# Hybrid Hyena and pooling encoder layer: the LayerNorm's gain and bias move from VectorE to GpSimd in the last stage

## The chip, the cores and the metric

The kernel runs on one core of a Trainium2 chip. The metric is the device time of one execution in microseconds (us), the median over runs. The engines named below are PE (TensorE, the matrix products), PEld (its weight loads), DVE (VectorE), ACT (ScalarE), POOL (GpSimd) and SP (SyncE, which issues the DMAs here).

## The reference

One encoder layer over x of 2048 x 1024 in fp32. One input projection feeds two branches, a two-fold gated long convolution and a pooling mixer; their outputs `y` (2048 x 1024) are mapped by one output matrix, gated, added to the scaled input, and normalised per row:

```python
ALPHA = DEEPNORM_ALPHA                      # 2 ** 0.25
def _layer_norm(x, g, b):
    mu = jnp.mean(xf, axis=-1, keepdims=True)
    var = jnp.mean(jnp.square(xf - mu), axis=-1, keepdims=True)
    y = (xf - mu) * lax.rsqrt(var + LN_EPS)
    return y * g + b
...
out = gate[:, None, :] * (y @ w_out[layer] + b_out[layer])
h = _layer_norm(DEEPNORM_ALPHA * h + out, ln_g[layer], ln_b[layer])
```

The change concerns only this last step.

## The kernel before

The layer runs in stages, each a block of its own with its buffers and semaphores: filters, input projection, three passes of a long convolution done as Fourier products, and at the end `last_inverse` and `output_norm`. Every product of two fp32 matrices is done as three products of parts (`mm3`, L150 to L152): a high part, and a low part that is what the high one leaves.

`output_norm` (from L1898) works on 16 tiles of 128 rows (tokens) by 1024 columns. Nearly every buffer is there twice, indexed by the tile number modulo 2. For tile n:

- ACT makes the high parts of `y` (`yhi`, `high`, L1975 and L1978), DVE the low parts (`ylo`, `low`, L1999 and L2002), each in two halves of 512 columns. They may overwrite the buffers once PE has finished tile n − 2.
- PE does 48 products into `ps` (`unit`): 24 that need the first half, then 24 that need the second.
- DVE makes `res` = ALPHA · x + gate bias beforehand (`skip`, L2009), and after PE's last product of the tile runs `norm`: it adds `ps` to `res` (L2025), takes the row statistics (L2029, L2032), then L2036 makes (res − mean) · ln_g while ACT takes the square root (`root`, L1983); five small instructions of one column (L2040 to L2044) refine the reciprocal, and L2048 makes o = res · rstd + ln_b.
- SP loads x (L1932) and stores `o` (L1944).

There is no scheduler: each engine's order is written out by `pipeline`, which walks over the tiles in bodies of four and gives for each body the steps with their lag. On DVE it is `[(low, 0), (skip, 0), (norm, 1)]`: low(n), skip(n), norm(n − 1), low(n + 1), and so on; behind the last tile only norms are left. On ACT it is high(n), root(n − 2), on SP load(n), store(n − 2). Waits are on semaphores only: `skip` waits for x and for `o_done` of tile n − 2 (since `res` is then free), the last instruction of `norm` also for the store of tile n − 2. POOL does one memset in this stage (`eps`, L1990). In the stage before, POOL makes the low part of the output weights (`whl`, L1867), and in the projection that of the input weights (L664, L666); these are the places where the trace shows POOL doing work of 128x1024.

Of the kernel before, what the change touches and what calls it, by code (L numbers as in the profile page):

```python
# [10 lines left out]
ALU = mybir.AluOpType  # L11
# [10 lines left out]
GS = L // P  # L22
# [132 lines left out]
def f32(ap):  # L155
    return ap.bitcast(F32)
# [9 lines left out]
def after(eng, sem, count):  # L166

    if not (isinstance(count, int) and count <= 0):
        eng.wait_ge(sem, count)


U = 4


def at(it, b, ring):

    it, b = it + b // U, b % U
    return b % ring, (U // ring) * it + b // ring


def pipeline(eng, units, steps, peel=(0,)):

    bodies = units // U
    steps = [step if len(step) == 3 else (*step, 2) for step in steps]
    first = max(1, *(-(-(lag + start) // U) for _, lag, start in steps))
    steps = [step[:2] for step in steps]

    def body(it, count=U):  # L190
        for b in range(count):
            for step, lag in steps:
                if not isinstance(it, int) or 0 <= U * it + b - lag < units:
                    step(it, b - lag)

    it = 0
    while it < bodies:
        if it < first or it in peel:
            body(it)
            it += 1  # L200
            continue
        end = min([p for p in peel if p > it] + [bodies])
        with eng.Fori(it, end) as i:
            body(i)
        it = end
    body(bodies, max(lag for _, lag in steps))
# [1691 lines left out]
def output_norm(nc, t, ya, yp, whl, gate_bias, out):  # L1898

    with Scope(nc, "out") as s:  # L1900
# [4 lines left out]
        res = [s.sb(f"res{b}", [P, D]) for b in range(2)]  # L1905
        o = [s.sb(f"o{b}", [P, D]) for b in range(2)]
        ln_g = s.sb("ln_g", [P, D])
        ln_b = s.sb("ln_b", [P, D])
        stats = [s.sb(f"stats{b}", [P, 2, 6]) for b in range(2)]
        mv = [s.sb(f"mv{b}", [P, 2]) for b in range(2)]  # L1910
        sm = [s.sb(f"sm{b}", [P, 4]) for b in range(2)]
        eps = s.sb("eps", [P, 1])
        ps = [s.ps(f"ps{b}", [P, 2, CH]) for b in range(2)]
        consts, eps_set = s.sem("consts"), s.sem("eps_set")
        yb_in = s.sems("yb_in", 4)
        x_in, hi_done, lo_done, mm_done, step, skip_done, sum_done, var_done, root_done, scaled, o_done, stored = (
            s.sems(n) for n in ("x_in", "hi_done", "lo_done", "mm_done", "step", "skip_done", "sum_done", "var_done",
                                "root_done", "scaled", "o_done", "stored"))
        block = s.block()

        @block.sync
        def _(sp):
            def load_yb(c):
                cols = slice(c * CH, (c + 1) * CH)
                sp.dma_start(yb[:, :, cols], yp[:, :, cols].rearrange("k p t -> p k t")).then_inc(yb_in[c], 16)

            def load(it, b):
                r, used = at(it, b, 2)
                after(sp, skip_done[r], used)
                row = P * (U * it + b)  # L1930
                src = t["x"][0, row:row + P, :] if isinstance(it, int) else t["x"][0, bass.ds(row, P), :]
                sp.dma_start(x[r][:, :], src).then_inc(x_in[r], 16)  # L1932
                if isinstance(it, int) and U * it + b == 1:
                    sp.dma_start(ln_g[:, :], t["ln_g"][0, :].partition_broadcast(P)).then_inc(consts, 16)
                    sp.dma_start(ln_b[:, :], t["ln_b"][0, :].partition_broadcast(P)).then_inc(consts, 16)
                    for c in range(1, 4):
                        load_yb(c)

            def store(it, b):
                r, used = at(it, b, 2)  # L1940
                sp.wait_ge(o_done[r], used + 1)
                row = P * (U * it + b)
                dst = out[0, row:row + P, :] if isinstance(it, int) else out[0, bass.ds(row, P), :]
                sp.dma_start(dst, o[r][:, :]).then_inc(stored[r], 16)  # L1944

            load_yb(0)
            pipeline(sp, GS, [(load, 0), (store, 2)])
            for r in range(2):
                sp.wait_ge(stored[r], 16 * GS // 2)
# [38 lines left out]
        @block.gpsimd  # L1988
        def _(pool):
            nc.gpsimd.memset(eps[:, :], LN_EPS).then_inc(eps_set, 1)  # L1990

        @block.vector
        def _(dve):
            def low(it, b):
                r, used = at(it, b, 2)
                cols = bass.ds(P * (U * it + b), P)
                dve.wait_ge(hi_done[r], 2 * used + 1)
                after(dve, mm_done[r], used)
                nc.vector.tensor_tensor(ylo[r][:, 0:4, :], ya[:, :, cols],  # L1999
                                        f32(yhi[r][:, 0:4, :]), ALU.subtract).then_inc(lo_done[r], 1)  # L2000
                dve.wait_ge(hi_done[r], 2 * used + 2)
                nc.vector.tensor_tensor(ylo[r][:, 4:8, :], yb[:, :, cols],  # L2002
                                        f32(yhi[r][:, 4:8, :]), ALU.subtract).then_inc(lo_done[r], 1)

            def skip(it, b):
                r, used = at(it, b, 2)
                dve.wait_ge(x_in[r], 16 * used + 16)
                after(dve, o_done[r], used)
                nc.vector.scalar_tensor_tensor(out=res[r][:, :], in0=x[r][:, :], scalar=ALPHA, in1=gate_bias[:, :],  # L2009
                                               op0=ALU.mult, op1=ALU.add).then_inc(skip_done[r], 1)  # L2010

            def norm(it, b):
                r, used = at(it, b, 2)
                STEPS = 6
                n = STEPS * used
                done = [0]

                def then(ins):
                    ins.then_inc(step[r], 1)
                    done[0] += 1  # L2020
                    dve.wait_ge(step[r], n + done[0])

                dve.wait_ge(skip_done[r], used + 1)
                dve.wait_ge(mm_done[r], used + 1)
                nc.vector.tensor_tensor(res[r][:, :], ps[r][:, :, :].rearrange("p a b -> p (a b)"), res[r][:, :],  # L2025
                                        ALU.add).then_inc(sum_done[r], 1)
                dve.wait_ge(sum_done[r], used + 1)
                for h in range(2):
                    ins = nc.vector.bn_stats(stats[r][:, h, :], res[r][:, h * CH:(h + 1) * CH])  # L2029
                then(ins)  # L2030
                nc.vector.memset(sm[r][:, 2:4], 0.0)
                nc.vector.bn_aggr(mv[r][:, :], stats[r][:, :, :].rearrange("p a b -> p (a b)")).then_inc(var_done[r], 1)  # L2032
                dve.wait_ge(var_done[r], used + 1)
                if isinstance(it, int) and U * it + b == 0:
                    dve.wait_ge(consts, 32)
                nc.vector.scalar_tensor_tensor(out=res[r][:, :], in0=res[r][:, :], scalar=mv[r][:, 0:1], in1=ln_g[:, :],  # L2036
                                               op0=ALU.subtract, op1=ALU.mult).then_inc(scaled[r], 1)
                dve.wait_ge(root_done[r], used + 1)

                then(nc.vector.reciprocal(sm[r][:, 1:2], sm[r][:, 0:1]))  # L2040
                then(nc.vector.tensor_scalar(sm[r][:, 2:3], mv[r][:, 1:2], LN_EPS, sm[r][:, 1:2], ALU.add, ALU.mult))  # L2041
                then(nc.vector.tensor_tensor(sm[r][:, 2:3], sm[r][:, 2:3], sm[r][:, 1:2], ALU.mult))  # L2042
                then(nc.vector.tensor_scalar(sm[r][:, 2:3], sm[r][:, 2:3], -0.5, 1.5, ALU.mult, ALU.add))  # L2043
                then(nc.vector.tensor_tensor(sm[r][:, 3:4], sm[r][:, 2:3], sm[r][:, 1:2], ALU.mult))  # L2044
                assert done[0] == STEPS
                dve.wait_ge(scaled[r], used + 1)
                after(dve, stored[r], 16 * used)
                nc.vector.scalar_tensor_tensor(out=o[r][:, :], in0=res[r][:, :], scalar=sm[r][:, 3:4], in1=ln_b[:, :],  # L2048
                                               op0=ALU.mult, op1=ALU.add).then_inc(o_done[r], 1)

            pipeline(dve, GS, [(low, 0), (skip, 0), (norm, 1)])


# [60 lines left out]
```

## Time and profile before

| | |
|---|---|
| median of 3 runs | 1349.3 us (1344.42, 1349.3, 1350.38) |
| the profiled execution | 1344.42 us, its span 1342.6 us |
| busy over the span | PE 1119.0, PEld 857.6, DVE 861.3, ACT 532.1, POOL 149.1 us |
| `output_norm` | from about 1148 us to the end of the span |
| in it, 1160 to 1310 us | PE 150.00 of 150 us busy, DVE 109.14, ACT 20.25, POOL 0 |
| last store issued | 1338.57 us |

A time of the timeline is the start of an instruction from the span's start and its length. On DVE the next instruction's start lies some 0.08 us before the end of the one in front, so the step from start to start is what an instruction costs there. A bracket behind a row is idle time before it and what ended it. An instruction that is held up once it has started shows this as a longer duration, not as idle time.

### The profile page before, as it was taken

Reading aid. Unit: us, or ns where it says so; the run is one execution under the profiler, and the core shown is the slowest. Engines: PE = TensorE matmul, PEld = TensorE weight load, DVE = VectorE, ACT = ScalarE, POOL = GpSimd, SP = SyncE. Lnnn points to the kernel's source line nnn. Section 1 sums busy time; section 2 is a strip of 40 time slices with the busy share of each in tenths; the row PEclk is TensorE's granted clock in tenths of the full one; section 3 lists DMA queues with packets and bytes.
Section 4 is the critical chain, followed back from the end, with each engine's and each line's share of the span. In section 5 each row is a group of like instructions: output and inputs, shape, how many; then the busy total and the mean of one; then the engine's idle time right before and its main releaser. Section 6 shows DMA issues by size and latency. Waiting matters only on the chain. (4 is left out here: it accounts for less than half of the span.)

```text
span 1342.6 us, 14415 instructions
## 1 busy us (share of the span) xinstructions
PE 1119.0 (83%) x4940; PEld 857.6 (64%) x4940; DVE 861.3 (64%) x1037; ACT 532.1 (40%) x722; POOL 149.1 (11%) x98
## 2 busy tenths in 40 slices
PE   3789746999999799969888499976999646899996
PEld 1257534788888577657666377754777434688885
DVE  5969659555545165548778355644888538577776
ACT  3347635333433133336565333333666435111110
POOL 0011044111111111111100111101110014100000
PEclk9879957999999799979999799997999869899999
DMA  8369998687653246587787567767798598622221
GB/s 299 111 207 354 317 253 279 206 267 260 214 189 115 71 130 194 172 209 230 234 238 231 152 175 228 244 214 206 232 276 257 161 373 282 235 94 94 94 94 47
DMA packets 156337, 276.56 MB, mean 206 GB/s; under 512 B 24743, under 2 KB 46375, under 8 KB 154154
## 3 DMA queue, kind: packets, MB, share of 16 engines
q1 hardware_dynamic: 151773, 269.60, 62.9%
q0 software_dynamic: 3168, 5.51, 1.5%
q8 instruction: 37, 0.61, 0.2%
q10 hardware_dynamic: 1328, 0.59, 0.2%
q14 instruction: 31, 0.25, 0.1%
HBM read 183.37 MB, written 98.57 MB: 210 GB/s over the span
## 5 line engine op out<-in xcount | busy, mean ns | idle before, releaser
L150 PE MATMUL prj_pp<-prj_uhi,prj_whi 128*128 128x512 f32 x768 | 308.6, 402 | 14.9 <-POOL prj_ulo L1044 8.7
L152 PE MATMUL prj_pp<-prj_uhi,prj_wlo 128*128 128x512 f32 x768 | 304.7, 397 | 0.0
L151 PE MATMUL prj_pp<-prj_ulo,prj_whi 128*128 128x512 f32 x768 | 304.6, 397 | 0.0
L150 PEld LDWEIGHTS prj_pp<-prj_uhi,prj_whi 128*128 128x128 f32 x768 | 147.5, 192 | 57.0 <-issue 25.4
L152 PEld LDWEIGHTS prj_pp<-prj_uhi,prj_wlo 128*128 128x128 f32 x768 | 146.7, 191 | 32.5
L151 PEld LDWEIGHTS prj_pp<-prj_ulo,prj_whi 128*128 128x128 f32 x768 | 147.0, 191 | 31.7
L150 PE MATMUL out_ps<-whl,out_yhi 128*128 128x512 f32 x256 | 102.5, 400 | 4.3 <-DVE out_ylo L1999 4.3
L151 PE MATMUL out_ps<-whl,out_yhi 128*128 128x512 f32 x256 | 102.2, 399 | 0.0
L152 PE MATMUL out_ps<-whl,out_ylo 128*128 128x512 f32 x256 | 102.1, 399 | 0.0
L664 POOL CAST prj_whi<-prj_ws 128x1024 fp32r<-128x1024 f32 x24 | 28.3, 1180 | 611.5 <-PE prj_pp L152 518.0
L1165 DVE TENSOR_TENSOR p_alo<-p_a,p_ahi 128x1024 fp32r<-128x1024 f32 x32 | 45.4, 1419 | 74.5 <-ACT p_ahi L1105 74.4
L1105 ACT ACTIVATE p_ahi<-p_a 128x1024 fp32r<-128x1024 f32 x32 | 33.9, 1060 | 118.0 <-PE p_ps L152 103.0
L1486 ACT ACTIVATE p_us<-p_u 64x512 f32<-64x512 f32 x64 | 38.1, 595 | 91.6 <-PE p_u L152 52.2
L150 PE MATMUL p_u<-p_ahi,p_fwd 128*128 128x512 f32 x64 | 28.9, 451 | 45.9 <-DVE p_alo L1528 29.7
L666 POOL TENSOR_TENSOR prj_wlo<-prj_ws,prj_whi 128x1024 fp32r<-128x1024 f32 x24 | 60.2, 2506 | 1.9
L150 PEld LDWEIGHTS out_ps<-whl,out_yhi 128*128 128x128 f32 x256 | 48.6, 190 | 16.4 <-DVE out_ylo L1999 4.5
L694 ACT ACTIVATE prj_row<-prj_pp,prj_b_in 128x512 f32<-128x512 f32 x64 | 43.4, 679 | 37.8 <-PE prj_pp L152 37.8
L535 PE MATMUL fs_s<-fs_khi,fs_tab 64*128 64x512 f32 x256 | 50.7, 416 | 7.7 <-ACT fs_xo L576 7.7
L1975 ACT ACTIVATE out_yhi<-ya 128x512 fp32r (+1 forms) x16 | 10.1, 631 | 117.6 <-PE out_ps L152 114.1
L151 PEld LDWEIGHTS out_ps<-whl,out_yhi 128*128 128x128 f32 x256 | 48.7, 190 | 12.0
L152 PEld LDWEIGHTS out_ps<-whl,out_ylo 128*128 128x128 f32 x256 | 48.7, 190 | 11.9
L1555 DVE TENSOR_TENSOR p_us<-p_us,p_k_im 128x1024 f32<-128x1024 f32 x32 | 39.2, 1226 | 20.6 <-ACT p_us L1487 20.6
(180 smaller groups left out, 2076.2 us busy)
## 6 DMA issues: line engine op xcount, KB each, us to landing
kseq<-fs_xo SPq DMA_DIRECT2D x32, 512.0 KB, 5.2
p_a<-kseq SPq DMA_DIRECT2D x32, 512.0 KB, 4.4
kfreq<-p_out SPq DMA_DIRECT2D x32, 512.0 KB, 5.2
xseq<-p_xo SPq DMA_DIRECT2D x32, 512.0 KB, 6.5
p_a<-xseq SPq DMA_DIRECT2D x32, 512.0 KB, 5.7
p_k_re<-kfreq SPq DMA_DIRECT2D x64, 256.0 KB, 4.1
p_k_im<-kfreq SPq DMA_DIRECT2D x64, 256.0 KB, 4.5
bseq<-p_out SPq DMA_DIRECT2D x32, 512.0 KB, 4.8
```

Source lines behind the costliest of these rows:

```text
L150: nc.tensor.matmul(out, w[0], m[0], start=start, stop=False, skip_group_check=True)
L151: nc.tensor.matmul(out, w[0], m[1], start=False, stop=False, skip_group_check=True)
L152: return nc.tensor.matmul(out, w[1], m[0], start=False, stop=stop, skip_group_check=True)
L535: mm = nc.tensor.matmul(s1_ps[r][:, jj, :], tab[g % 3][js, h, a, :], m[r3][js, h, :], start=h == 0 and part == 0, stop=h == 1 and part == ...
L664: self.nc.gpsimd.tensor_copy(self.whi[b][:, :, :], self.ws[:, :, :]).then_inc(self.whi_done[b], 1)
L666: self.nc.gpsimd.tensor_tensor(self.wlo[b][:, :, :], self.ws[:, :, :], f32(self.whi[b][:, :, :]), ALU.subtract).then_inc(self.wlo_done[b], 1)
L694: self.nc.scalar.activation(self.row[:, PAD + c * CH:PAD + (c + 1) * CH], self.pp[q % 2][:, :], ACT.Identity, bias=self.b_in[:, col:col + ...
L1105: nc.scalar.activation(ahi[:, :, :], a[n % 2][:, :, :], ACT.Copy).then_inc(hi_done, 1)
L1165: nc.vector.tensor_tensor(alo[:, :, :], a[n % 2][:, :, :], f32(ahi[:, :, :]), ALU.subtract).then_inc(lo_done, 1)
L1486: nc.scalar.activation(us[0:64, i, :], u_ps[64:128, i, :], ACT.Copy, scale=-1.0)
L1555: nc.vector.tensor_tensor(us[:, :, :], us[:, :, :], k_im[:, :, :], ALU.mult).then_inc(turn_done, 1)
L1975: nc.scalar.activation(yhi[r][:, 0:4, :], ya[:, :, cols], ACT.Copy).then_inc(hi_done[r], 1)
```

## The change

Of the four factors of (res − mean) · rstd · ln_g + ln_b, DVE keeps the first two in one instruction, tensor_scalar in place on `res` with the two column operands mean and rstd, and raises the new semaphore `norm_done`. POOL multiplies by ln_g into `o` (raises `scaled`), waits for its own multiply, and adds ln_b in place (raises `o_done`). The two scalar_tensor_tensor instructions of DVE are gone. POOL takes over the wait for the constants and for the store of tile n − 2. `skip` waits for `scaled` (POOL has read `res`) and no longer for `o_done`.

```diff
         @block.gpsimd
         def _(pool):
             nc.gpsimd.memset(eps[:, :], LN_EPS).then_inc(eps_set, 1)
+            pool.wait_ge(eps_set, 1)
+            pool.wait_ge(consts, 32)
+            for n in range(GS):
+                b, it = n % 2, n // 2
+                pool.wait_ge(norm_done[b], it + 1)
+                after(pool, stored[b], 16 * it)
+                nc.gpsimd.tensor_tensor(o[b][:, :], res[b][:, :], ln_g[:, :], ALU.mult).then_inc(scaled[b], 1)
+                pool.wait_ge(scaled[b], it + 1)
+                nc.gpsimd.tensor_tensor(o[b][:, :], o[b][:, :], ln_b[:, :], ALU.add).then_inc(o_done[b], 1)
@@ skip
                 dve.wait_ge(x_in[r], 16 * used + 16)
-                after(dve, o_done[r], used)
+                after(dve, scaled[r], used)
@@ norm
                 nc.vector.bn_aggr(mv[r][:, :], stats[r][:, :, :].rearrange("p a b -> p (a b)")).then_inc(var_done[r], 1)
-                dve.wait_ge(var_done[r], used + 1)
-                if isinstance(it, int) and U * it + b == 0:
-                    dve.wait_ge(consts, 32)
-                nc.vector.scalar_tensor_tensor(out=res[r][:, :], in0=res[r][:, :], scalar=mv[r][:, 0:1], in1=ln_g[:, :],
-                                               op0=ALU.subtract, op1=ALU.mult).then_inc(scaled[r], 1)
                 dve.wait_ge(root_done[r], used + 1)
...
-                dve.wait_ge(scaled[r], used + 1)
-                after(dve, stored[r], 16 * used)
-                nc.vector.scalar_tensor_tensor(out=o[r][:, :], in0=res[r][:, :], scalar=sm[r][:, 3:4], in1=ln_b[:, :],
-                                               op0=ALU.mult, op1=ALU.add).then_inc(o_done[r], 1)
+                nc.vector.tensor_scalar(res[r][:, :], res[r][:, :], mv[r][:, 0:1], sm[r][:, 3:4],
+                                        ALU.subtract, ALU.mult).then_inc(norm_done[r], 1)
```

DVE, one tile of `output_norm` before, from the statistics of tile n − 1 to the sum of tile n (`sm` holds the small columns, `mv` mean and variance):

```order
L2032 BN_AGGR out_mv<-out_stats 128x2
L2036 SCALAR_TENSOR_TENSOR out_res<-out_res,out_mv,out_ln_g 128x1024
L2040 RECIPROCAL out_sm<-out_sm 128x1
L2041 TENSOR_SCALAR out_sm<-out_mv,out_sm 128x1
L2042 TENSOR_TENSOR out_sm<-out_sm 128x1
L2043 TENSOR_SCALAR out_sm<-out_sm 128x1
L2044 TENSOR_TENSOR out_sm<-out_sm 128x1
L2048 SCALAR_TENSOR_TENSOR out_o<-out_res,out_sm,out_ln_b 128x1024
L1999 TENSOR_TENSOR out_ylo<-ya,out_yhi 128x512
L2002 TENSOR_TENSOR out_ylo<-out_yb,out_yhi 128x512
L2009 SCALAR_TENSOR_TENSOR out_res<-out_x,gate_bias 128x1024
L2025 TENSOR_TENSOR out_res<-out_ps,out_res 128x1024
```

The same piece of DVE's order in the changed kernel, whose lines lie 9 further down where the text is the same up to the statistics:

```order
L2041 BN_AGGR out_mv<-out_stats 128x2
L2044 RECIPROCAL out_sm<-out_sm 128x1
L2045 TENSOR_SCALAR out_sm<-out_mv,out_sm 128x1
L2046 TENSOR_TENSOR out_sm<-out_sm 128x1
L2047 TENSOR_SCALAR out_sm<-out_sm 128x1
L2048 TENSOR_TENSOR out_sm<-out_sm 128x1
L2050 TENSOR_SCALAR out_res<-out_res,out_mv,out_sm 128x1024
L2008 TENSOR_TENSOR out_ylo<-ya,out_yhi 128x512
L2011 TENSOR_TENSOR out_ylo<-out_yb,out_yhi 128x512
L2018 SCALAR_TENSOR_TENSOR out_res<-out_x,gate_bias 128x1024
L2034 TENSOR_TENSOR out_res<-out_ps,out_res 128x1024
```

Between the statistics and the reciprocal nothing stands any more; the tensor_scalar stands where L2048 stood, with the low halves and the skip product right behind it.

POOL, in the same stage, the first two tiles of the changed kernel and what is in front:

```order
L1990 MEMSET out_eps 128x1
L1997 TENSOR_TENSOR out_o<-out_res,out_ln_g 128x1024
L1999 TENSOR_TENSOR out_o<-out_o,out_ln_b 128x1024
L1997 TENSOR_TENSOR out_o<-out_res,out_ln_g 128x1024
L1999 TENSOR_TENSOR out_o<-out_o,out_ln_b 128x1024
```

Before, the memset was all; now 32 instructions of 128x1024 follow it.

## Rows read from the trace of the kernel before

**Rows 1.** 1160 to 1310 us: length, PE, PEld, DVE, ACT, POOL busy, clock, DMA

```profile
1160.00:1310.00 150.00, 150.00 (x644) 120.49 (x643) 109.14 (x196) 20.25 (x41) 0.00 (x0) 1.00 0.32 112
```

**Rows 2.** waits, 1010 to 1343 us: engine, line, releaser, total, times, longest

```profile
DVE out_res L2025 <- PE out_ps L152: 45.5, 16, 5.7
...
PE out_ps L150 <- DVE out_ylo L1999: 4.3, 1, 4.3
```

**Rows 3.** timeline of DVE, one tile: start us, us, engine, line, shapes, [idle before]

```profile
1265.02 1.22 DVE L2025 TENSOR_TENSOR out_res<-out_ps,out_res 128x1024 f32<-128x1024 f32 x1 [2.53 <-PE out_ps L152]
...
1267.60 0.20 DVE L2032 BATCH_NORM_AGGREGATE out_mv<-out_stats 128x2 f32<-128x12 f32 x1
...
1267.84 1.29 DVE L2036 SCALAR_TENSOR_TENSOR out_res<-out_res,out_mv,out_ln_g 128x1024 f32<-128x1024 f32 x1
1269.04 0.16 DVE L2040 RECIPROCAL out_sm<-out_sm 128x1 f32<-128x1 f32 x1
...
1270.06 1.29 DVE L2048 SCALAR_TENSOR_TENSOR out_o<-out_res,out_sm,out_ln_b 128x1024 f32<-128x1024 f32 x1
1271.26 0.69 DVE L1999 TENSOR_TENSOR out_ylo<-ya,out_yhi 128x512 fp32r<-128x512 f32 x1
1271.86 0.68 DVE L2002 TENSOR_TENSOR out_ylo<-out_yb,out_yhi 128x512 fp32r<-128x512 f32 x1
1272.47 1.22 DVE L2009 SCALAR_TENSOR_TENSOR out_res<-out_x,gate_bias 128x1024 f32<-128x1024 f32 x1
1276.21 1.22 DVE L2025 TENSOR_TENSOR out_res<-out_ps,out_res 128x1024 f32<-128x1024 f32 x1 [2.53 <-PE out_ps L152]
```

**Rows 4.** timeline of ACT, same tile: the square root

```profile
1267.84 0.29 ACT L1983 ACTIVATE out_sm<-out_mv,out_eps 128x1 f32<-128x1 f32 x1 [1.64 <-DVE out_mv L2032]
```

**Rows 5.** one line's instructions, L392: duration ns min/median/max

```profile
L392 DVE TENSOR_SCALAR net_arg<-net_arg x6: 693/694/694, 21.4 to 57.9; 128x1024 f32<-128x1024 f32 x6
```

**Rows 6.** the same view for L712

```profile
L712 DVE TENSOR_SCALAR prj_cv<-prj_row,prj_cw,prj_cb x48: 531/541/2419, 223.1 to 1044.0; 128x512 f32<-128x512 f32 x48
```

**Rows 7.** timeline of POOL at the end of the stage before, L1867

```profile
1139.64 3.21 POOL L1867 TENSOR_TENSOR whl<-fin_wf,whl 128x1024 fp32r<-128x1024 f32 x1 [3.39 <-ACT whl L1858]
1145.09 2.37 POOL L1867 TENSOR_TENSOR whl<-fin_wf,whl 128x1024 fp32r<-128x1024 f32 x1 [2.25 <-ACT whl L1858]
```

**Rows 8.** page, part 5: POOL's two-input instructions of the projection

```profile
L666 POOL TENSOR_TENSOR prj_wlo<-prj_ws,prj_whi 128x1024 fp32r<-128x1024 f32 x24 | 60.2, 2506 | 1.9
```

**Rows 9.** timeline of DVE, the last tile

```profile
1332.21 1.23 DVE L2025 TENSOR_TENSOR out_res<-out_ps,out_res 128x1024 f32<-128x1024 f32 x1 [4.87 <-PE out_ps L152]
...
1337.26 1.28 DVE L2048 SCALAR_TENSOR_TENSOR out_o<-out_res,out_sm,out_ln_b 128x1024 f32<-128x1024 f32 x1
```

**Rows 10.** timeline of all engines, the end: the last store

```profile
1338.57 0.34 SPq L1944 DMA_DIRECT2D out<-out_o  x1
```

**Rows 11.** timeline of DVE around 1140 us, beside POOL of rows 7

```profile
1139.38 1.21 DVE L1876 TENSOR_TENSOR fin_xlo<-fin_x,fin_xhi 128x1024 fp32r<-128x1024 f32 x1
1140.51 1.08 DVE L1884 TENSOR_TENSOR ya<-fin_tps,ya 128x512 f32<-128x512 f32 x1
1141.49 2.43 DVE L1892 TENSOR_TENSOR fin_wf<-fin_wf,fin_gate 128x1024 f32<-128x1024 f32 x1
```

**Rows 12.** timeline of all engines at 660 us: POOL and DVE take turns

```profile
660.39 1.22 DVE L1528 TENSOR_TENSOR p_alo<-p_a,p_ahi 128x1024 fp32r<-128x1024 f32 x1
...
660.44 2.06 POOL L664 CAST prj_whi<-prj_ws 128x1024 fp32r<-128x1024 f32 x1 [37.22 <-PE prj_pp L152]
...
661.52 1.26 DVE L712 TENSOR_SCALAR prj_cv<-prj_row,prj_cw,prj_cb 128x512 f32<-128x512 f32 x1
...
662.58 2.47 POOL L666 TENSOR_TENSOR prj_wlo<-prj_ws,prj_whi 128x1024 fp32r<-128x1024 f32 x1
...
662.82 2.78 DVE L715 SCALAR_TENSOR_TENSOR prj_cv<-prj_row,prj_cw,prj_cv 128x512 f32<-128x512 f32 x1
```

**Rows 13.** DMA issues, 1145 to 1343 us: KB each, median us to landing

```profile
out_x<-in_x SPq DMA_DIRECT2D x16, 512.0 KB, 3.9
```

More of the change, by code:

```diff
@@ L1915, in output_norm @@
         yb_in = s.sems("yb_in", 4)
-        x_in, hi_done, lo_done, mm_done, step, skip_done, sum_done, var_done, root_done, scaled, o_done, stored = (
+        x_in, hi_done, lo_done, mm_done, step, skip_done, sum_done, var_done, root_done, norm_done, scaled, o_done, stored = (
             s.sems(n) for n in ("x_in", "hi_done", "lo_done", "mm_done", "step", "skip_done", "sum_done", "var_done",
-                                "root_done", "scaled", "o_done", "stored"))
+                                "root_done", "norm_done", "scaled", "o_done", "stored"))
         block = s.block()
```

## The prediction, made before the changed kernel was run

> **What bounds the kernel now.** The change touches only the last stage, so I first read the busy time of that stage. From 1160 to 1310 us TensorE is busy for all of the 150.00 us, at a granted clock of 1.00 (2.4 GHz), VectorE for 109.14 and POOL for none [rows 1]. Then the list of waits: in the whole stage PE waited once for VectorE's low halves, 4.3 us, at the start (`ylo`, L1999), while VectorE waited 16 times, 45.5 us in all, for PE's product [rows 2]. So the stage goes at PE's pace. The timeline of VectorE gives this pace: the sum of one tile (L2025) starts at 1265.02 and that of the next at 1276.21, 11.19 us a tile, the last 2.53 us of them idle [rows 3]. What can move the end is (a) what stands behind PE's last product, since nothing hides it, and (b) VectorE's loop, if it needs more than 11.19 us a tile for long enough that PE waits for `ylo`. The first is a plain sum. The second is close, and decides how far above the sum the result lies.
>
> **The serial part of a tile on VectorE, before.** I call S the start of a tile's sum. The square root on ACT and the removed L2036 both start at S + 2.82 (1267.84 less 1265.02) [rows 3, 4]. The five small instructions from L2040 to L2044 take 1270.06 − 1269.04 = 1.02 us [rows 3].
>
> **Removed.** Two instructions a tile, L2036 and L2048, 1.29 us each, 1.20 from start to start [rows 3]. L2036 covered the square root: that took 0.29 [rows 4], so it was ready long before 1269.04. Without the cover the reciprocal waits for it: it starts at about S + 2.82 + 0.29 + 0.04 for the signal (0.04 is also what lay between the end of L2032, 1267.80, and ACT's start [rows 3, 4]) = S + 3.15, and the small ones end at S + 4.17.
>
> **Added on VectorE.** One tensor_scalar of 128x1024, in place, one tensor in, two [128,1] operands. The trace has no such form. The nearest rows are the same width with constants, 0.694 us [rows 5], and half the width with two column operands, 0.541 [rows 6]. Twice the width costs a two-input instruction 1.22 − 0.68 = 0.54 us more [rows 3]; L392 does 1024 elements in what those need for 512, so it goes at twice their rate, and I add 0.27: 0.54 + 0.27 = 0.81. I take 0.80. From below it is bounded by 0.69, from above by the 1.29 of the removed form. So it ends at S + 4.97, where the removed L2048 ended at S + 6.33.
>
> A rule that bears on this choice, of the Trainium skill, VectorE: DVE Perf Modes, "The perf-mode tier table": an fp32 tensor_scalar from SBUF to SBUF runs at two elements a cycle, and a tensor_tensor at one. L392 agrees with it, and by it the new instruction is nearer to 0.8 than to 1.29.
>
> **Added on POOL.** Two tensor_tensor of 128x1024 a tile, each behind a semaphore. POOL's own two-input instruction of this size took 2.37 us where nothing was in its way [rows 7]; the 24 of the projection averaged 2.51, waiting included [rows 8]. I take 2.37, and 2.37 to 2.5 as bounds. With about 0.06 for VectorE's signal and 0.09 between the two the pair ends 4.9 us behind the tensor_scalar.
>
> The Trainium skill, GPSIMD Engine Reference, "Performance versus the Vector engine", speaks against moving such work: a two-input elementwise instruction costs GpSimd about 2.6 cycles an element, and VectorE one. By its rate, 1024 x 2.6 / 1.2 GHz = 2.2 us (estimate from that page), the tail's +3.5 below would be +3.2; the row stands at 2.37, so it is used.
>
> **The tail (a), the main term.** Before, the last tile's sum starts at 1332.21, L2048 starts at 1337.26 and ends 1.28 later, 1338.54, so 6.33 us from S, and the store is issued at 1338.57 [rows 9, 10]. After: S + 4.97 + 0.06 + 2.37 + 0.09 + 2.37 = S + 9.86, and then the same store. Difference +3.5 us. Bounds: 0.69 and 2.37 give +3.4; 0.81 and 2.5 give +3.8. A tensor_scalar of 1.29 adds 0.5.
>
> **The loop (b).** What was hidden work becomes contention. Where POOL's two-input instruction meets a two-input instruction of VectorE, the trace shows one waiting for the whole of the other. At 1139.38 VectorE runs L1876 for 1.21; POOL's, begun at 1139.64, takes 3.21 instead of 2.37, so it ends 2.26 behind VectorE's end, at 1142.85; VectorE's next two-input one, L1892, begun at 1141.49, takes 2.43 instead of 1.22 and ends at 1143.92, 1.07 behind POOL's [rows 7, 11]. L1884 between them, whose one input is PSUM, ran beside POOL in 1.08 [rows 11]. And they take turns: around 660 us VectorE asks at 660.39, POOL at 660.44, VectorE at 661.52 with L712 (a tensor_scalar, 1.26 instead of 0.54), POOL at 662.58, VectorE at 662.82, and each gets its turn in this order [rows 12]. So even back-to-back instructions of VectorE let a waiting POOL in between.
>
> In the changed kernel what follows the tensor_scalar on VectorE is just of that kind: `ylo` first half, `ylo` second half, the skip product (both inputs in SBUF, 0.69, 0.68 and 1.22 [rows 3]). Counted from the tensor_scalar's end, with a blocked instruction ending its own time less 0.14 behind the other's end (2.37 − 2.23; 0.68 − 0.55; both rounded [rows 7, 11, 12]):
> - low half 1, already running: ends at +0.60
> - POOL's multiply, asked for meanwhile: +0.60 + 2.23 = +2.83
> - low half 2: +2.83 + 0.55 = +3.38
> - POOL's add, asked for at +2.9: +5.61
> - the skip product, which must also wait for the multiply, is behind the add: +5.61 + 1.08 = +6.69; the next sum can start 0.08 earlier, +6.61.
>
> A tile needs 4.97 + 6.61 = 11.58 us on VectorE, against PE's 11.19. So VectorE, which had 2.53 us to spare, falls back by 0.39 us a tile. That does not reach PE at once: PE's next tile needs the first `ylo` half, which is ready at S + 4.97 + 0.60 = S + 5.57, when VectorE is not late, and is wanted at S + 11.19: 5.62 us of room. The last tile that PE takes gets its `ylo` behind the norm of tile 13; by then VectorE is 13 x 0.39 = 5.1 us late. So PE just doesn't wait, by half a microsecond. At the end there are no more low halves and skips, and VectorE catches up: tile 14's norm ends 5.5 + 4.97 = 10.5 behind its product, before the last product at 11.19. But POOL's pair of tile 14 then lasts until about 4.1 us into the last tile's norm, where the small two-input instructions (L2042, L2044 before) may be blocked for up to 0.5 us. Term: 0 to +0.5, I take +0.2.
>
> **Others, at nothing.** The skip product's wait for `scaled` instead of `o_done` is inside the turns above. On SP the store moves later by some 4 us, and the load behind it; x takes 3.9 us to land [rows 13] and is used more than 9 us after its issue, so it stays hidden, and if that cover went, the skip product would be late by the difference. On ACT only the root is behind VectorE; the high halves wait for PE alone.
>
> **Sum.** 3.5 + 0.2 = +3.7 us. The profiled execution took 1344.42 us (span 1342.6, 1.8 outside it), so 1348.1 for it. That run is the lowest of the three shown; on the median of 1349.3 it is 1353.0, +0.27%. What a measurement of this kernel can tell from no change is about 0.5%, 6.7 us, so I forecast "no change that can be told", on the slow side.
>
> **Rivals.**
> - No queueing that counts: VectorE keeps the port through its back-to-back instructions, or POOL asks later. The loop is then 4.97 + 0.60 + 0.60 + 2.23 + about 1.2 = 9.6 us, below 11.19, and only the tail is left: +3.5, 1352.8. Against it: POOL got in between at 661.5 [rows 12].
> - The loop is longer than read, slower than before beyond what can be told (other side, the first of two sizes): each 0.1 us more a tile costs PE 1.3 us as soon as the lateness passes 5.62. With POOL at 2.5 the loop is 0.26 longer, 0.65 late a tile: 13 x 0.65 − 5.6 = 2.8 us of waiting PE, and with the pair at 2.5 and the blocking +7 in all, 1356. From 0.43 a tile on it decides. For it: the mean of 2.51 [rows 8]; against it: the undisturbed 2.37 [rows 7].
> - The tensor_scalar at the removed form's 1.29 us: loop 12.07, 0.88 late a tile, past 5.62 after seven tiles, 13 x 0.88 − 5.6 = 5.8 us of waiting PE; tail 3.5 + 0.5; POOL's pair of tile 14 blocks the small instructions for some 1.2 more: +11, 1360. For it: two column operands are only seen at 512. Against it: 0.541 there is less than the 0.68 of a one-rate instruction [rows 3, 6].
> - Faster: PE has no gap to give back and the tail only grows, so only run-to-run difference would show it (1344.4 to 1350.4 in the runs shown).
>
> **How the numbers follow.** Forecast, +3.5 to +5: 0.52. First rival 0.15. Longer loop, +5 to +10: 0.18. Slow tensor_scalar, +11 or more: 0.10. The rest 0.05. Below 6.7 us lie the forecast, the first rival and a bit of the third: with the runs' own spread, same 0.70; slower 0.26; faster 0.04. The range goes from 1348 (tail alone on a run as low as the profiled one) to 1360 (slow tensor_scalar on the median).
>
> **What would show it.** The norm's tensor_scalar at 0.80; POOL busy about 5 us a tile, more in the records since they hold its waiting; the second `ylo` half and the skip product of VectorE stretched to some 3 us and 3.5 us; VectorE's idle time before the sum gone, and the sum starting later behind the product from tile to tile, by about 0.4; PE still without waits; from the last sum to the store 9.9 us. Wrong would be: PE waiting for `ylo` in the second half of the stage (longer loop), idle time still before each sum (first rival), or a shorter tail.

## The result, and the profile after

| | before | changed |
|---|---|---|
| median | 1348.01 us (1342.95 to 1350.38, 8 runs) | 1354.88 us (1350.19 to 1357.9, 8 runs) |
| profiled execution | 1344.42 us, span 1342.6 | 1355.51 us, span 1353.7 |
| first sum of the last stage starts at | 1164.22 | 1170.51 |
| from there to the last sum | 167.99 | 168.87 |
| from the last sum to the last store's issue | 6.36 | 10.28 |
| from there to the end of the span | 4.03 | 4.04 |
| the stage: from the first sum to the end | 178.38 | 183.19 |

The ratio of the changed kernel to the one before is 1.0056, with a 95% interval of 1.0035 to 1.0077: slower, by about the least that can be told. The stage that was changed takes 4.8 us more, 0.36%. Of the 11.1 us between the two spans 6.3 stand ahead of the first sum, where the two programs are the same; the experiments show how far that time wanders by itself.

Busy time between 1160 and 1310 us in the changed kernel, with the columns of [rows 1]:

```profile
1160.00:1310.00 150.00, 150.00 (x641) 120.39 (x640) 136.27 (x173) 21.50 (x42) 66.12 (x24) 0.99 0.32 114
```

VectorE has two instructions of 128x1024 a tile fewer and one more, and is busy for 136 us instead of 109 [rows 1]. That is the first lesson of this text: busy time also counts the time for which an instruction is held. The waits of the last stage (who waited, for whom, us in all, times, longest):

```profile
DVE out_res L2034 <- PE out_ps L152: 6.1, 2, 5.4
...
PE out_ps L150 <- DVE out_ylo L2008: 4.5, 2, 4.3
```

Before each sum VectorE used to wait for PE, 45.5 us over 16 tiles [rows 2]. Now it waits twice: at the first and at the last tile. PE, on the other hand, has one wait more in the list than the 4.3 at the start. The chain of work that ended last ran mostly through PE before (PE 14% of the span, DVE 1%); now it runs mostly through VectorE:

```profile
DVE 9%; issue 3%; PE 2%; ACT 0%; DVEq 0%; POOL 0%; POOLq 0%
```

### The profile page after: what moved, and what is told of

It is laid out like the page before. It is cut to its first block and busy times, and to the rows that moved or that the text cites. A ratio compares the mean times of both kernels' runs of the same rounds, so it can differ in the third digit from the quotient of the medians.

```text
span 1353.7 us, 14426 instructions
## 1 busy us (share of the span) xinstructions
PE 1128.5 (83%) x4940; PEld 863.8 (64%) x4940; DVE 895.4 (66%) x1021; ACT 532.4 (39%) x722; POOL 234.9 (17%) x130
## 5 line engine op out<-in xcount | busy, mean ns | idle before, releaser
L1997 POOL TENSOR_TENSOR out_o<-out_res,out_ln_g 128x1024 f32<-128x1024 f32 x16 | 43.6, 2722 | 106.9 <-DVE out_res L2050 106.9
```

Of the source, the lines that this page charges most:

```text
L1997: nc.gpsimd.tensor_tensor(o[b][:, :], res[b][:, :], ln_g[:, :], ALU.mult).then_inc(scaled[b], 1)
```

## Where the 4.8 us are

One tile in the middle, the timeline of DVE and POOL together, answering to [rows 3]:

```profile
1193.84 1.21 DVE L2034 TENSOR_TENSOR out_res<-out_ps,out_res 128x1024 f32<-128x1024 f32 x1
...
1196.41 0.20 DVE L2041 BATCH_NORM_AGGREGATE out_mv<-out_stats 128x2 f32<-128x12 f32 x1
...
1196.98 0.16 DVE L2044 RECIPROCAL out_sm<-out_sm 128x1 f32<-128x1 f32 x1 [0.36 <-ACT out_sm L1983]
...
1198.00 0.81 DVE L2050 TENSOR_SCALAR out_res<-out_res,out_mv,out_sm 128x1024 f32<-128x1024 f32 x1
...
1198.73 0.68 DVE L2008 TENSOR_TENSOR out_ylo<-ya,out_yhi 128x512 fp32r<-128x512 f32 x1
1198.89 2.78 POOL L1997 TENSOR_TENSOR out_o<-out_res,out_ln_g 128x1024 f32<-128x1024 f32 x1 [6.07 <-DVE out_res L2050]
...
1199.33 2.90 DVE L2011 TENSOR_TENSOR out_ylo<-out_yb,out_yhi 128x512 fp32r<-128x512 f32 x1
...
1201.75 2.73 POOL L1999 TENSOR_TENSOR out_o<-out_o,out_ln_b 128x1024 f32<-128x1024 f32 x1
...
1202.15 3.42 DVE L2018 SCALAR_TENSOR_TENSOR out_res<-out_x,gate_bias 128x1024 f32<-128x1024 f32 x1
...
1205.49 1.21 DVE L2034 TENSOR_TENSOR out_res<-out_ps,out_res 128x1024 f32<-128x1024 f32 x1
```

Read the durations against [rows 3]: the second `ylo` half takes 2.90 instead of 0.68, the skip product 3.42 instead of 1.22. POOL's multiply asks at 1198.89, while the first half runs, gets in when that is done at 1199.41 and ends 2.26 later; the second half, asked for at 1199.33, ends 0.56 behind it; then the add, then the skip product. From sum to sum it is 11.66 us (1205.49 less 1193.84, with rounding), PE's pace being 11.20. There is no idle time before the sum. The tensor_scalar takes 0.81, and the reciprocal starts 3.14 us behind the sum.

So VectorE falls back by 0.46 us a tile, and near the end PE feels it. Tiles are counted from 0 here. The starts of PE's tiles 14 and 15, the last two, timeline of all engines:

```profile
1315.36 0.68 DVE L2008 TENSOR_TENSOR out_ylo<-ya,out_yhi 128x512 fp32r<-128x512 f32 x1
...
1315.60 0.39 PE L152 MATMUL out_ps<-whl,out_ylo 128*128 128x512 f32 x1
...
1316.10 0.50 PE L150 MATMUL out_ps<-whl,out_yhi 128*128 128x512 f32 x1
...
1327.00 0.69 DVE L2008 TENSOR_TENSOR out_ylo<-ya,out_yhi 128x512 fp32r<-128x512 f32 x1
...
1327.17 0.40 PE L152 MATMUL out_ps<-whl,out_ylo 128*128 128x512 f32 x1
...
1327.83 0.47 PE L150 MATMUL out_ps<-whl,out_yhi 128*128 128x512 f32 x1 [0.26 <-DVE out_ylo L2008]
```

Inside a tile PE's products start 0.23 us apart. The first of tile 14 starts 0.50 behind the one in front of it, just after the end of the `ylo` half that it needs (1316.04), and the second follows after 0.34. The first of tile 15 starts 0.66 behind the one in front, 0.14 after the end of its half (1327.69), and the second follows after 0.31. What is above 0.23 adds up to 0.27 + 0.11 + 0.43 + 0.08 = 0.89 us, and from the first to the last sum the stage is 0.88 us longer than before. So PE was held twice, and that is the whole of this part. The list of waits shows only 0.2 of it, because a product's record is 0.39 to 0.40 long, longer than the step to the next: as idle time a short hold shows too small or not at all.

The traces also say when the half is wanted. In the kernel before, the timeline of PE has the first product of the next tile at 1275.95, where the sum in [rows 3] starts at 1276.21. PE begins the next tile 0.26 us ahead of the sum of the one in front. The prediction had it wanting the half at the sum + 11.19, so the room for VectorE's lateness is not 5.62 us but 5.36. The half of tile 14 is made behind the norm of tile 12, and by then VectorE is 12 x 0.46 = 5.52 us late, past 5.36. For tile 13 it was 11 x 0.46 = 5.06, and PE wasn't held.

The last tile, timeline of all engines, answering to [rows 9], and SP's last store, answering to [rows 10]:

```profile
1339.38 1.23 DVE L2034 TENSOR_TENSOR out_res<-out_ps,out_res 128x1024 f32<-128x1024 f32 x1 [0.67 <-PE out_ps L152]
...
1341.21 2.34 POOL L1999 TENSOR_TENSOR out_o<-out_o,out_ln_b 128x1024 f32<-128x1024 f32 x1
...
1342.98 0.59 DVE L2046 TENSOR_TENSOR out_sm<-out_sm 128x1 f32<-128x1 f32 x1
...
1343.99 0.81 DVE L2050 TENSOR_SCALAR out_res<-out_res,out_mv,out_sm 128x1024 f32<-128x1024 f32 x1
1344.88 2.34 POOL L1997 TENSOR_TENSOR out_o<-out_res,out_ln_g 128x1024 f32<-128x1024 f32 x1 [1.33 <-DVE out_res L2050]
1347.30 2.34 POOL L1999 TENSOR_TENSOR out_o<-out_o,out_ln_b 128x1024 f32<-128x1024 f32 x1
```

```profile
1349.66 0.34 SPq L1944 DMA_DIRECT2D out<-out_o  x1
```

The tensor_scalar ends at the sum + 5.42, POOL's pair at + 10.26. One small instruction, L2046, has two inputs of one column in SBUF; it takes 0.59 instead of 0.16, held until the add of tile 14 ends at 1343.55. From the last sum to the last store's issue it is 3.92 us longer than before; I call this part the tail. 0.88 + 3.92 = 4.8.

## The experiments

Each ran beside the kernel before on the same chip (29 runs of it for e1 to e4, 23 for e5 to e7), with 12 runs of its own, e4 with 6 and e6 with 4. "The stage" is the time from the first sum to the end of the span, 178.4 before. It and the two columns in front are read from one profile of each; the changed kernel was profiled twice, with 183.2 and 183.3.

| run | from sum to sum | first to last sum | the stage | ratio to before (95%) |
|---|---|---|---|---|
| before | 11.20 | 168.0 | 178.4 | |
| changed | 11.66 | 168.9 | 183.2 | 1.0056 (1.0035 to 1.0077) |
| e1, changed again | 11.66 | 168.9 | 183.3 | 1.0025 (1.0006 to 1.0044) |
| e2, last tile on VectorE | 11.66 | 168.9 | 180.5 | 1.0019 (1.0002 to 1.0037) |
| e3, only the last tile on POOL | 11.20 | 168.0 | 182.1 | 1.0028 (1.0012 to 1.0044) |
| e4, multiply behind the low halves | 12.20 | 176.0 | 190.9 | 1.0086 (1.0051 to 1.0120) |
| e5, add behind the skip product | 11.20 | 168.0 | 182.0 | 1.0028 (1.0011 to 1.0046) |
| e6, one more tensor_scalar | 12.38 | 179.0 | 194.9 | 1.0115 (1.0086 to 1.0144) |
| e7, all on VectorE, split last tile | 11.20 | 167.9 (right half) | 177.0 | 0.9982 (0.9965 to 0.9998) |

**e1: the changed kernel again**, no edit.

> The changed kernel once more, beside the other variants. Theory A (what the traces show of the last stage is all): from the first sum to the issue of the last store it takes 179.2 us as in the first profile, before 174.4, so the kernel is 4.8 us slower, +0.36%, and the first sum's own time (1164.2 before, 1170.5 after in the two profiles) differs only from run to run. Rival B (the stages ahead of the change have become slower too, as the two profiles and the median difference of 6.9 us suggest): +0.5% or more again, and the first sum again some 6 us later than in before.

Median 1351.28 us of 12 runs, against 1347.94 of 29. The stage takes 183.3 us, to a tenth what it took the first time, while the first sum is back at 1165.0. Over the nine profiles of this text it started at 1163.3 to 1166.6, and twice at 1170.5 (in the changed kernel and in e6), in programs that are the same up to there. So nothing shows that the stages ahead became slower; the first measurement's 0.56% and this one's 0.25% lie on both sides of the stage's 0.36%, which is inside both intervals. What makes the time ahead of the stage wander stays open: the two profiles' mean granted clock was 0.928 before and 0.920 in the changed kernel, but over the 52 runs of the kernel before that stood beside the experiments, clock and time go together only loosely.

**e2: the last tile on VectorE.** POOL's loop runs over GS − 1 tiles, and `norm` of the last tile is the one before, with waits for POOL and for the store of tile 13 (cut here):

```diff
-            for n in range(GS):
+            for n in range(GS - 1):
@@ norm, last tile only
+                    nc.vector.scalar_tensor_tensor(out=res[r][:, :], in0=res[r][:, :], scalar=mv[r][:, 0:1], in1=ln_g[:, :],
+                                                   op0=ALU.subtract, op1=ALU.mult).then_inc(scaled[r], 1)
...
+                    nc.vector.scalar_tensor_tensor(out=o[r][:, :], in0=res[r][:, :], scalar=sm[r][:, 3:4], in1=ln_b[:, :],
+                                                   op0=ALU.mult, op1=ALU.add).then_inc(o_done[r], 1)
```

> Tiles 0 to 14 as in the changed kernel, the last tile's gain and bias on VectorE as before. Theory A: the loop of 11.66 us a tile stays, VectorE 5 to 6 us late at tile 14; from the last sum to the last store it takes not 10.3 but 6.3 plus about 1.2, since the two-input instruction with ln_g asks at the sum + 2.8 and POOL's add of tile 14 goes on until + 4.2: 7.5. So 2.7 us less than the changed kernel, first sum to store 176.5. Rival (the loss lies in the loop, VectorE's lateness, not in the tail): no gain over the changed kernel, first sum to store 178 to 179. Rival (no waiting behind POOL at the end): the tail is 6.3.

Timeline of all engines, the last tile:

```profile
1333.42 1.23 DVE L2034 TENSOR_TENSOR out_res<-out_ps,out_res 128x1024 f32<-128x1024 f32 x1 [0.64 <-PE out_ps L152]
...
1335.30 2.34 POOL L1999 TENSOR_TENSOR out_o<-out_o,out_ln_b 128x1024 f32<-128x1024 f32 x1
...
1336.25 2.47 DVE L2046 SCALAR_TENSOR_TENSOR out_res<-out_res,out_mv,out_ln_g 128x1024 f32<-128x1024 f32 x1
...
1339.66 1.28 DVE L2060 SCALAR_TENSOR_TENSOR out_o<-out_res,out_sm,out_ln_b 128x1024 f32<-128x1024 f32 x1
```

From the last sum to the last store's issue it is 7.5 us: the instruction with ln_g is held by POOL's add of tile 14 until 1337.64 and takes 2.47 instead of 1.28. The stage is 2.7 us shorter than the changed kernel's. The tail is real, and part of what is won by taking the last tile off POOL is lost because POOL is still at tile 14.

**e3: only the last tile on POOL**, the kernel before otherwise (the same edit the other way round).

> The kernel before, only the last tile's gain and bias on POOL. Theory A: no loop with turns, VectorE waits 2.5 us for PE at each tile as before; the last sum to the store takes 3.15 + 1.02 + 0.81 + 0.06 + 2.35 + 0.08 + 2.35 = 9.8 us, 3.5 more than before; first sum to store 177.9, time +3.5 us, +0.26%. Rival (loss in the loop): no slower than before.

Timeline of all engines, the last tile, sum and POOL's pair:

```profile
1334.61 1.22 DVE L2033 TENSOR_TENSOR out_res<-out_ps,out_res 128x1024 f32<-128x1024 f32 x1 [4.87 <-PE out_ps L152]
...
1339.84 2.34 POOL L1996 TENSOR_TENSOR out_o<-out_res,out_ln_g 128x1024 f32<-128x1024 f32 x1 [188.44 <-DVE out_res L2062]
1342.26 2.34 POOL L1998 TENSOR_TENSOR out_o<-out_o,out_ln_b 128x1024 f32<-128x1024 f32 x1
```

One tile out of 16 moved, and three quarters of the loss are there: 3.7 us of 4.8. From sum to sum it stays at 11.20. The pair ends 9.99 behind the sum, 0.2 more than expected.

**e4: the multiply behind the low halves.**

```diff
                 pool.wait_ge(norm_done[b], it + 1)
+                if n + 2 < GS:
+                    pool.wait_ge(lo_done[b], 2 * it + 4)
```

> The changed kernel, but POOL's multiply waits until VectorE has made both low halves of the tile two further on, so POOL no longer gets in between them. Theory A: the second low half takes 0.68 again; the skip product waits for the multiply (2.35, plus signals), the add runs beside the sum; the loop is 4.98 + 0.6 + 0.6 + 2.5 + 1.2 = 9.9 us a tile, below PE's 11.2, so VectorE is never late and has 1.3 us idle at each tile; nothing of POOL's tile 14 is left when the last norm's small instructions run; last sum to store 9.8, first sum to store 177.9: 1.3 us less than the changed kernel and like e3. Rival (VectorE's lateness costs nothing at all, everything is the tail): the same time as the changed kernel within 0.5 us. Rival (turns do not matter for the order): the second low half still takes 2.9.

This missed by far, and in the other direction: ratio 1.0086. Timeline of DVE and POOL, one tile:

```profile
1183.57 0.69 DVE L2013 TENSOR_TENSOR out_ylo<-out_yb,out_yhi 128x512 fp32r<-128x512 f32 x1
...
1184.40 2.39 POOL L1999 TENSOR_TENSOR out_o<-out_res,out_ln_g 128x1024 f32<-128x1024 f32 x1 [7.34 <-DVE out_ylo L2013]
...
1186.87 2.40 POOL L2001 TENSOR_TENSOR out_o<-out_o,out_ln_b 128x1024 f32<-128x1024 f32 x1
1186.90 3.45 DVE L2020 SCALAR_TENSOR_TENSOR out_res<-out_x,gate_bias 128x1024 f32<-128x1024 f32 x1 [2.64 <-POOL out_o L1999]
...
1190.28 1.21 DVE L2036 TENSOR_TENSOR out_res<-out_ps,out_res 128x1024 f32<-128x1024 f32 x1
```

The low halves are free again, 0.69. But the skip product has to wait for the multiply, and when that is done both engines ask again: POOL's add at 1186.87, VectorE's skip product at 1186.90. The add goes first, and the skip product takes 3.45; so it is at all 14 skip products that wait for a multiply, with the add 0.02 to 0.03 ahead. I had it the other way round. Half the turns are gone, yet the loop has become longer, 12.20, since the multiply no longer overlaps anything that VectorE can do. VectorE is then 1.00 late a tile, and PE waits for it nine times, at the start (4.3) and at each tile from tile 8 on:

```profile
PE out_ps L150 <- DVE out_ylo L2010: 10.2, 9, 4.3
```

**e5: the add behind the skip product.**

```diff
                 pool.wait_ge(scaled[b], it + 1)
+                if n + 2 < GS:
+                    pool.wait_ge(skip_done[b], it + 2)
```

> The changed kernel, but POOL's add waits until VectorE has made the skip product of the tile two further on. Theory A (a tile's loop on VectorE against PE's 11.20 us decides, and in e4 the loop was 12.20 because POOL's add, asking 0.02 us ahead of the skip product, still went first): the multiply gets in between the low halves, the second of them takes 2.9; the skip product takes 1.22 again, the add runs beside the sum. Loop 4.98 + 0.6 + 2.25 + 0.47 + 1.2 = 9.5 us, below 11.20: 1.7 us of idle time before each sum, PE never waits, first sum to last sum 168.0, last sum to the end of the store's issue 10.4 as in e3, span behind the first sum 182.1: 1.1 less than the changed kernel (183.2), 3.7 more than before (178.4). Rival (POOL's work costs by its amount, not by its turns): as the changed kernel, 183.2.

Timeline of DVE and POOL, one tile:

```profile
1192.02 2.78 POOL L1997 TENSOR_TENSOR out_o<-out_res,out_ln_g 128x1024 f32<-128x1024 f32 x1 [4.17 <-DVE out_res L2052]
...
1192.45 2.90 DVE L2013 TENSOR_TENSOR out_ylo<-out_yb,out_yhi 128x512 fp32r<-128x512 f32 x1
...
1195.27 1.21 DVE L2020 SCALAR_TENSOR_TENSOR out_res<-out_x,gate_bias 128x1024 f32<-128x1024 f32 x1
...
1196.62 2.42 POOL L2001 TENSOR_TENSOR out_o<-out_o,out_ln_b 128x1024 f32<-128x1024 f32 x1 [1.83 <-DVE out_res L2020]
...
1198.14 1.23 DVE L2036 TENSOR_TENSOR out_res<-out_ps,out_res 128x1024 f32<-128x1024 f32 x1 [1.66 <-PE out_ps L152]
```

The multiply still holds the second low half (2.90), the skip product is free (1.21), and the add runs beside the sum and the statistics, which it does not slow. VectorE waits 1.66 us for PE before the sum, PE never for VectorE, and the stage takes 182.0, the value of e3. The same amount of POOL's work, differently placed, costs nothing but the tail.

**e6: one more tensor_scalar in each norm**, in front of the one with mean and rstd:

```diff
+                then(nc.vector.tensor_scalar(res[r][:, :], res[r][:, :], 1.0, 0.0, ALU.mult, ALU.add))
```

> The changed kernel with one more tensor_scalar of 128x1024 with constants (times 1, plus 0) in each norm, about 0.7 us. Theory A (threshold: VectorE's loop minus 11.20 adds up until its lateness passes 5.6 us, then PE waits for it): loop 11.66 + 0.72 = 12.38, 1.18 late a tile, PE's first wait at the fifth or sixth tile, 13 x 1.18 - 5.6 = 9.7 us of waiting in all; tail + 0.72; span behind the first sum 183.2 + 9.7 - 0.3 + 0.7 + about 0.6 for more blocking at the end = 194. Rival (each tile's extra work counts at once): 16 x 0.72 = 11.5, 194.7, but then with PE waiting from the second tile on. Rival (VectorE hidden as before): + 0.7, 183.9.

The loop is 12.38 us. PE's waits in the stage, and the first of them behind the start that the list has, at tile 7:

```profile
PE out_ps L150 <- DVE out_ylo L2008: 12.8, 10, 4.3
```

```profile
1238.85 0.47 PE L150 MATMUL out_ps<-whl,out_yhi 128*128 128x512 f32 x1 [1.02 <-DVE out_ylo L2008]
```

By the steps between the products PE is held first at the start of tile 6 (1226.37, 0.42 behind the product in front instead of 0.23, too short for the list). That is a tile or two later than I had written. For six tiles the lateness costs nothing, then about all of it: the threshold of theory A. The totals can't tell it from the rival that counts each tile's work at once (194 and 194.7 expected, 194.9 measured); the waits can, since the rival had PE waiting from the second tile on.

My 9.7 us for PE's side was 1.3 short of the 11.0 measured, and the traces show where that lies. The added instruction stands in front of the low half too and takes 0.72 off the room; PE wants the half 0.26 earlier than I had it; and at the last hold the first product starts 0.14 behind the half and the second 0.08 late, as in the changed kernel. So the room is 5.36 − 0.72 = 4.64, and 13 x 1.18 − 4.64 + 0.22 = 10.9. The same sum gives 13 x 0.46 − 5.36 + 0.22 = 0.84 for the changed kernel, where 0.88 was measured, and 13 x 1.00 − 5.36 + 0.22 = 7.9 for e4, against 8.0. It also gives the first tile at which PE is held, 14, 8 and 6, as in the traces.

**e7: a version for the tail.** The experiments say that in this stage, as long as VectorE keeps PE's pace, only what stands behind PE's last product counts. So this version leaves all on VectorE, as before, and shortens that. PE's last four tiles are written out, so that the last one can be told apart; declarations and the code of the stores are left out here:

```diff
@@ unit, last tile: behind the left half's last product
+                            mm.then_inc(left_done, 1)
@@ norm, last tile
+                    for h, (sem, value) in enumerate(((left_done, 1), (mm_done[r], used + 1))):
+                        cols = slice(h * CH, (h + 1) * CH)
+                        dve.wait_ge(sem, value)
+                        nc.vector.tensor_tensor(res[r][:, cols], ps[r][:, h, :], res[r][:, cols],
+                                                ALU.add).then_inc(sum_done[r], 1)
+                        dve.wait_ge(sum_done[r], used + 1 + h)
+                        ins = nc.vector.bn_stats(stats[r][:, h, :], res[r][:, cols])
...
+                for cols in ((slice(0, CH), slice(CH, D)) if last else (slice(0, D),)):
+                    nc.vector.scalar_tensor_tensor(out=o[r][:, cols], in0=res[r][:, cols], scalar=sm[r][:, 3:4],
+                                                   in1=ln_b[:, cols], op0=ALU.mult, op1=ALU.add).then_inc(o_done[r], 1)
@@ store, last tile: two halves of the columns, each behind its o_done
```

> The kernel before, all on VectorE, but in the last tile the sum and the statistics of the left half of the columns are made as soon as PE has finished that half (12 products, 2.8 us, before its last), and the last instruction and the store go in two halves. Theory A (what stands behind PE's last product is all that can be won in this stage): the sum and statistics left behind the last product are half as long, 1.2 us less; the last instruction's halves cost 0.1 more together, and the store's second half lands a bit sooner than the whole: span behind the first sum 178.4 - 1.2 - 0 to 0.5 = 176.7 to 177.3, time -1 to -1.7 us, -0.1%, which the median can hardly tell but the trace can. Rival (the end is set by the store of 512 KB, not by VectorE): no gain.

Timeline of DVE and SP, the last tile:

```profile
1328.45 0.69 DVE L2037 TENSOR_TENSOR out_res<-out_ps,out_res 128x512 f32<-128x512 f32 x1 [2.07 <-PE out_ps L152]
...
1329.17 0.69 DVE L2040 BATCH_NORM_STATS2 out_stats<-out_res 128x6 f32<-128x512 f32 x1
...
1331.18 0.69 DVE L2037 TENSOR_TENSOR out_res<-out_ps,out_res 128x512 f32<-128x512 f32 x1 [1.31 <-PE out_ps L152]
1331.91 0.69 DVE L2040 BATCH_NORM_STATS2 out_stats<-out_res 128x6 f32<-128x512 f32 x1
...
1335.10 1.41 DVE L2067 SCALAR_TENSOR_TENSOR out_o<-out_res,out_sm,out_ln_b 128x512 f32<-128x512 f32 x2
1335.88 0.34 SPq L1946 DMA_DIRECT2D out<-out_o  x1
1336.57 0.33 SPq L1948 DMA_DIRECT2D out<-out_o  x1
```

The left half's sum and statistics (1328.45, 1329.17) are done before PE's last product; behind that come the right half's, 0.69 each. The stage takes 177.0 us, 1.4 less than before: 1.0 from PE's last product to the last store's issue, and 0.4 behind that issue, which is now of 256 KB instead of 512. The median is 1345.19 of 12 runs against 1348.01 of 23, ratio 0.9982 (0.9965 to 0.9998), the only version here that is faster than the kernel before, by about as little as can be told.

## Why the prediction was right, point by point

- **What bounds.** Right: PE sets the pace; what is behind its last product goes straight into the time. e3 shows it alone.
- **VectorE's serial part.** The reciprocal at S + 3.15: 3.14. The tensor_scalar 0.80: 0.81. Its end at S + 4.97: the same in a middle tile (1198.00 + 0.81 − 1193.84 = 4.97).
- **The tail.** Forecast +3.5, and 0 to 0.5 for the small instructions behind POOL's last pair but one, of which I took 0.2. Measured +3.92: the held L2046 adds 0.43, the pair 2.34 and 2.34 instead of twice 2.37. The mechanism was the one named, the size at the end of its range.
- **The turns.** The order (half, multiply, half, add, skip product) came as written, with 2.90 and 3.42 where I had "some 3 and 3.5". The loop was 11.66 instead of 11.58, and most of this was in the rows: rows 7 and 11 have POOL end 2.26 behind VectorE, and I put 2.23 into the sum, twice. With 2.26 it is 11.64.
- **The term that was off.** "So PE just doesn't wait, by half a microsecond": that step failed, though by little. The lateness was 0.46 a tile instead of 0.39, 6.0 us after 13 tiles, and the room was 5.36 instead of 5.62, since PE begins its next tile ahead of the sum. So PE's side, put at nothing, cost 0.88. With it and the 0.43 the sum would have been 4.8 instead of 3.7.
- **The time itself.** 1353.0 was forecast and 1354.88 measured, but the 1349.3 that I started from was the median of three runs; of eight it is 1348.01. The difference to before was forecast as 3.7. The stage shows 4.8, the second measurement 3.3, and the first 6.9, of which the stage does not explain the last 2. That 1353.0 came so near is in part luck.
- **The class.** I gave 0.70 to "no change that can be told" and 0.26 to slower; the first measurement says 0.56%, the second 0.25%, the stage in the profile 0.36%. Which of them one sees depends on the runs; my line of 0.5% ran through the middle of it.
- **The rivals.** "No queueing that counts" is wrong for this order, but e5 comes to the same loop below PE's pace with one wait and to the same cost: the tail alone, 3.6 above before, where this rival had 3.5. "The loop is longer than read" holds in kind with a small size. The slow tensor_scalar didn't occur.

## What to carry to other kernels

Where one engine sets the pace, as PE does here, work moved off another engine wins nothing, and what the move adds to the last instance is paid in full (e3): count first what stands behind the pacing engine's last instruction, since that is also where something can be won (e7). And when the helper and the engine that it relieves hold each other up, compare the relieved engine's whole loop, with these waits in it, with the pace: a lateness smaller than the slack in front costs nothing, and past it all of it. Read the slack from the pacing engine's own starts, and its holds from the steps between them. Where the two meet can be moved by one semaphore, for better (e5) or for worse (e4).

## What the runs showed of the hardware that I had not expected

- Taking one meeting away made things worse. The engine whose record starts 0.03 us earlier went first (e4: 1186.87 against 1186.90), and that decided 2.2 us a tile.
- An instruction on one column is held too. L2046, two inputs of 128x1, took 0.16 us alone, 0.59 in the changed kernel's last tile and 1.34 in e6's, where the tensor_scalar on one column right in front of it took its usual 0.21 beside the same POOL instruction:

```profile
1352.79 0.21 DVE L2045 TENSOR_SCALAR out_sm<-out_mv,out_sm 128x1 f32<-128x1 f32 x1
1353.03 1.34 DVE L2046 TENSOR_TENSOR out_sm<-out_sm 128x1 f32<-128x1 f32 x1
```

- POOL's two-input instruction took 2.34 us in the changed kernel's last tile, both with VectorE's statistics beside it (1341.21) and with VectorE done (1347.30): the statistics, one input in SBUF, did not touch it.
